# Square roots ahead of an exponential, and two products ahead of a barrier, in a one-core DeltaNet and short-convolution step

## The reference, cut to what matters

```
q, k = l2norm(silu(conv(x W_q))), l2norm(silu(conv(x W_k)));  v = silu(conv(x W_v));  z = x W_z
norm of a token  = sqrt(sum(t*t) + eps)            # per head, q and k
decay            = exp(gc_i - gc_j)                # inside the triangular inverse of each chunk
S, o             = gated delta rule over chunks (prompt), over 8 tokens (each sample)
o                = rmsnorm(o) * norm_g * silu(z)
y                = o @ w_out                       # "the mixer's output projection"
x                = layer_norm(ALPHA * x + y)
```

## Time and profile before

| what | value |
|---|---|
| median of 3 runs | 1735.3 us |
| the profiled execution | 1735.66 us, of which the span is 1733.6 us |
| PE busy | 1692.2 us, 98% |
| DVE busy | 1075.4 us, 62% |
| ACT busy | 460.7 us, 27% |
| POOL busy | 241.5 us, 14% |
| mean granted clock of PE | 0.995 of full speed |

### The profile page before, as it was taken

The page is one execution under the profiler, slowest core; times in us unless marked ns, Lnnn a source line. Parts: engine busy times, 40 slices in busy tenths (PEclk is TensorE's granted clock), DMA queues, the critical chain, the costliest instruction groups (busy, mean ns, idle before and its releaser), DMA issues. The chain is left out here.

```text
span 1733.6 us, 22781 instructions
## 1 busy us (share of the span) xinstructions
PE 1692.2 (98%) x8243; PEld 1321.8 (76%) x8243; DVE 1075.4 (62%) x2062; ACT 460.7 (27%) x1084; POOL 241.5 (14%) x537
## 2 busy tenths in 40 slices
PE   8999999999899999999999999999999999999999
PEld 5777678877677777777777777776777777777777
DVE  4866775676876766662336655468766667633375
ACT  2433406742422222210033111114222222200051
POOL 0111216652110000001100000012100000001100
PEclk9999999989999999999999999999999999999999
DMA  4232210331222222242140322211222222321211
GB/s 155 74 115 87 82 61 14 111 124 37 72 73 79 79 86 73 74 144 83 50 135 1 115 80 83 75 49 50 73 73 74 85 78 81 139 96 67 86 49 55
DMA packets 45645, 139.40 MB, mean 80 GB/s; under 512 B 4944, under 2 KB 12240, under 8 KB 45536
## 3 DMA queue, kind: packets, MB, share of 16 engines
q1 hardware_dynamic: 42864, 133.36, 23.6%
q10 hardware_dynamic: 2672, 4.61, 0.8%
HBM read 129.63 MB, written 8.31 MB: 80 GB/s over the span
## 5 line engine op out<-in xcount | busy, mean ns | idle before, releaser
L274 PE MATMUL bank<-z,ring 128*128 128x288 f32 x1952 | 509.5, 408 | 10.2 <-DVE z L392 2.8
L274 PEld LDWEIGHTS bank<-z,ring 128*128 128x128 f32 x1952 | 370.9, 191 | 117.8 <-issue 8.0
L274 PE MATMUL bank<-x,ring 128*128 128x288 f32 x1632 | 428.0, 409 | 11.4 <-DMA x<-in_x 4.9
L274 PEld LDWEIGHTS bank<-x,ring 128*128 128x128 f32 x1632 | 310.3, 191 | 102.0 <-issue 6.6
L2191 DVE SCALAR_TENSOR_TENSOR scratch<-scratch 128x592 f32<-128x592 f32 x176 | 146.2, 832 | 25.6 <-ACT scratch L2135 24.0
L274 PE MATMUL bank<-y,ring 128*128 128x288 f32 x616 | 156.4, 406 | 0.0
L274 PE MATMUL bank<-big,ring 128*128 128x288 f32 x536 | 137.8, 412 | 4.5 <-PEq L1774 2.3
L274 PEld LDWEIGHTS bank<-y,ring 128*128 128x128 f32 x616 | 117.0, 190 | 32.3
L274 PEld LDWEIGHTS bank<-big,ring 128*128 128x128 f32 x536 | 102.9, 193 | 35.4 <-issue 5.0
L2135 ACT ACTIVATE scratch<-scratch 128x592 f32<-128x592 f32 x88 | 69.4, 789 | 90.7 <-DVE scratch L2165 89.1
L2225 POOL COPY scratch<-scratch 128x2 f32<-128x2 f32 x88 | 26.0, 296 | 465.8 <-ACT scratch L2121 465.8
(11 more groups left out here) (372 smaller groups left out, 2172.4 us busy)
## 6 DMA issues: line engine op xcount, KB each, us to landing
ring<-in_w_up SPq DMA_DIRECT2D x88, 512.0 KB, 3.6
ring<-in_w_scin SPq DMA_DIRECT2D x24, 512.0 KB, 3.6
ring<-in_w_qkv SPq DMA_DIRECT2D x21, 512.0 KB, 3.6
ring<-in_w_down SPq DMA_DIRECT2D x12, 704.0 KB, 4.1
scratch<-in_w_down SPq DMA_DIRECT2D x12, 704.0 KB, 5.4
ring<-in_w_z SPq DMA_DIRECT2D x8, 512.0 KB, 3.6
big<-in_st_S SPq DMA_DIRECT2D x16, 256.0 KB, 6.0
out_dn_S_sample<-big SPq DMA_DIRECT2D x16, 256.0 KB, 3.0
```

The lines of the kernel that those rows point to most:

```text
L274: last = pe.matmul(bank[:, 0:HALF], w[:, k * P:(k + 1) * P], rhs(k), start=start and k == 0, stop=k == self.depth - 1, skip_group_check=no ...
```

## The change

Three edits. First, on ScalarE in block 1, the three square roots now stand ahead of the Exp of the inverse's decay. Second, the first products p1(0) and p1(1) of the output projection go from the head of block 3 to the end of block 2's TensorE order, behind the last update. They read 288 prompt columns and weights that block 1 loaded. Third, to keep banks 0 and 1 free for them, the updates of heads 6 and 7 and the second turn use other banks, and wait for other states.

```diff
-        UPDATE_BANKS = ((0, 1), (2, 3), (0, 1), (2, 3), (4, 5), (6, 7), (2, 3), (4, 5))
+        UPDATE_BANKS = ((0, 1), (2, 3), (0, 1), (2, 3), (4, 5), (6, 7), (4, 5), (6, 7))
+        TURN_BANKS = (0, 2)
...
-                pe.wait_ge(self.s_out, nth_update(2, 1))
+                pe.wait_ge(self.s_out, nth_update(3, 0))
                 self.turn_pe(pe, 1)
-                pe.wait_ge(self.s_out, nth_update(3, 1))
+                pe.wait_ge(self.s_out, nth_update(4, 1))
                 self.update_pe(pe, 6)
-                pe.wait_ge(self.s_out, nth_update(4, 1))
+                pe.wait_ge(self.s_out, nth_update(5, 1))
                 self.update_pe(pe, 7)
...
-            act.wait_ge(i_arg, NBL + 1)
-            act.activation(INV_G, INV_G, ACT.Exp).then_inc(i_expd, 1)
             act.wait_ge(turned, 1)
             act.activation(NRM[:, 0:NCH, :], BANK[6][:, 0:NCH * NT].rearrange("p (c m) -> p c m", m=NT), ACT.Sqrt
                            ).then_inc(rooted, 1)
             for part, c in ((slice(0, SAMP), NCH), (slice(SAMP, P), NCH + 1)):
                 act.activation(NRM[part, NCH, :], BANK[6][part, c * NT:(c + 1) * NT], ACT.Sqrt).then_inc(rooted, 1)
+            act.wait_ge(i_arg, NBL + 1)
+            act.activation(INV_G, INV_G, ACT.Exp).then_inc(i_expd, 1)
...
+        dout_first = Dense(NPAIR, KH, ring_set, lambda i, block: ring_loaded(uses[2] + 1, i, block),
+                           lambda k: BIG[:, 3 * k + 1, :], None, 0)
...
                 prompt.pe(pe)
                 samples.pe(pe)
+                dout_first.p1(pe, 0)
+                dout_first.p1(pe, 1)
...
         def mixer_pe(pe):
-            end_products(pe, dout, None, None, lambda pe: None, None)
+            d = dout
+            d.p2(pe, 0)
+            d.p2(pe, 1)
+            for i in range(2):
+                d.p6(pe, i)
+            for i in range(2):
+                d.p7(pe, i)
+            for i in range(2):
+                d.p4(pe, i)
+            end_products_late(pe, d)
             norm[0].sums(pe, 0)
             end_products_last(pe, dout)
```

More of the change, by code:

```diff
@@ L888, in turn_pe @@
                 for h in range(group * GROUP, (group + 1) * GROUP):
-                    last = pe.transpose(SBANK[group][:, h % GROUP * SAMP:(h % GROUP + 1) * SAMP], S_OS[B, h, :], IDENT[B, B])
+                    last = pe.transpose(SBANK[TURN_BANKS[group]][:, h % GROUP * SAMP:(h % GROUP + 1) * SAMP], S_OS[B, h, :], IDENT[B, B])
                 last.then_inc(self.o_turned, 1)
@@ L976, in gate_dve @@
                 dve.scalar_tensor_tensor(out=BIG[:, 1:QKV_T:3, SEQ:TOK][:, heads], scalar=norm_g,
-                                         in0=SBANK[group][:, 0:GROUP * SAMP].rearrange("p (h t) -> p h t", h=GROUP),
+                                         in0=SBANK[TURN_BANKS[group]][:, 0:GROUP * SAMP].rearrange("p (h t) -> p h t", h=GROUP),
                                          in1=Z[:, heads, SEQ:TOK], op0=ALU.mult, op1=ALU.mult).then_inc(self.o_gated, 1)
```

## The result

Before 1735.3 us (5 runs, 1732.45 to 1737.86), after 1742.0 us (5 runs, 1740.11 to 1742.41): ratio 1.0035, 95% interval [1.0023, 1.0047]. The change makes the kernel slower by 0.2 to 0.5%. The profiled execution took 1742.41 us (span 1740.5), 6.9 us of span more than the one of before. Ten more runs of the changed kernel, taken later beside 33 of the kernel before, gave 1740.05 against 1735.06, ratio 1.003 [1.0019, 1.004].

A forecast was written before the change was run, and what follows sets the result against it. TensorE, busy 98% of the span, was taken to bound the kernel. 1735.66 - 0.67 + 0 + 3.75 = 1738.7, less 0.4 to the median: 1738.4 us; own range 1737.6 to 1739.4, whole range 1734.9 to 1741.2.

The forecast's parts named there:

- rival 1: Block 3: the clock falls again behind TensorE's new gap, costing 1.7 us more, 1740.1 us; chance 0.22.
- Edit 2, 0: End of the samples' rule: new banks and waits hold up no update; cost 0, at most 0.4 us.
- Edit 3, +3.75: Second barrier: early products open it later, VectorE's u1(0) comes late, p7(0) waits; +3.75 us, between +1.55 and +5.45.
- The clock behind the new idle time: Block 3, behind TensorE's 3.8 us gap: forecast counts no clock fall; a fall would cost 1.7 us.
- Edit 1, -0.67: Block 1 grams: roots fit ScalarE's idle time, TensorE's wait for them goes; -0.67 us, between -2.4 and 0.
- rival 5: Block 1 grams: moving the roots gives nothing, the issue gap being fixed in time; 1739.1 us, chance 0.10.
- Rival 4: Second barrier: products fill TensorE's 2.26 us stand and the clock rises 1.7 us earlier; 1730.7 us, chance 0.07.

The follow-up runs named there:

- e3: Kernel before with only the other banks and waits for the updates of heads 6 and 7 and the second turn: 1735.7 us, ratio 0.9999.
- e2: Kernel before with the other banks and waits and the two products ahead of the barrier, square roots left behind the exponential: 1739.81 us, ratio 1.0023.
- e5: Changed kernel with VectorE's six weight sums of pairs 0 and 1 also ahead of the barrier: 1733.06 us, ratio 0.9992 to the kernel before.
- e4: Changed kernel with six extra unused matmuls in TensorE's gap before p7(0): 1739.93 us, ratio 1.0021 to the kernel before.
- e1: Kernel before with only the square roots moved ahead of the exponential on ScalarE: 1735.91 us against 1736.16, ratio 1.0.
- e7: Kernel before with dense matmuls between all three groups of 64 gram records: median 1731.08 us from 1734.37, ratio interval [0.9972, 1.0035].
- e6: Kernel before with only the first 64 gram records split off by dense matmuls, 128 left in a row: 1736.63 us, ratio 1.0007.
- e8: Changed kernel with both p2, ScalarE's copies of p1, six weight sums and all 16 token sums also ahead of the barrier: 1735.07 us, ratio 0.9999.
- e11: Changed kernel with p2, ScalarE's copies, weight sums and p6's token sums ahead of the barrier, other token sums behind u1(1): 1734.25 us, ratio 0.9997.
- e10: Changed kernel with VectorE's six weight sums ahead of the barrier and dense matmuls between the three gram groups: 1728.9 us, ratio 0.9968 to the kernel before.
- e12: Changed kernel with VectorE's sums divided around the barrier, p2 and copies ahead, and grams spread among dense matmuls: 1729.26 us, ratio 0.9965.

## Why the prediction was wrong

The result, 1742.0 us, lies above the range (1734.9 to 1741.2); the median of the later runs, 1740.05, lies within it, near rival 1 (1740.1). Whether the time fell inside or outside was thus partly chance; the step that failed below is seen in the traces of both.

- **Edit 2, 0.** Right: e3 shows no change, and in the traces of after and e3 no wait of the updates appears. In e2, where the updates ran at full clock, one waits 0.28 us; the prediction had up to 0.4 for that case.
- **Edit 3, +3.75.** Right in mechanism and size. The products took 5.99 us (6.1 predicted), the barrier opened at 388.8, of which 0.8 came from block 1, u1(0) came 13.8 us behind it, and TensorE waited 3.66 for it (3.8 predicted). p7(0) starts at 402.75, less 0.8 it is 3.9 later than 398.05. That the size fits so well is partly luck: it holds where the updates run at half clock, and in e2, where they didn't, it is 2.8. e5 shows the cause: with the six sums ahead of the barrier the loss goes.
- **The clock behind the new idle time: the step that failed.** The forecast had no fall there, and gave it to rival 1 at 0.22. It fell, in the traces of after (both) and of e2, and e4 sizes it at 1.6 to 1.7 us, as the rival had it. The comparison that I leant on was the stretch at 457 in the earlier trace rows, with 1.79 us of matmuls in 3.4. No idle time there is longer than 1.78 us, so it was no likeness of a gap of 3.8. Nor is it a place where the clock is sure to stay up: behind the same waits it falls in four of the 14 traces (0.54 from 459 to 462 us in e1, 0.50 from 453 to 456 in e7, and in e4 and e6). The nearer row was the fall at 214.8, behind a stand of 3.06 us in dense work, like the new gap. The Trainium skill, "TensorE: Matmul & The Clock Gate", section "Why this matters for your kernels", warns of such pauses, and the traces agree in this place.
- **Edit 1, -0.67.** The working on ScalarE was right: the roots fit in its idle time, and the exponential stayed at 206.3. The value was wrong: rival 5 (0.10), the wait gives nothing because the stand ends when it does, took place, and beyond it the low clock lasted longer, +0.8 in the trace of after, where the end of the range for this edit was 0. In medians e1 shows nothing either way.

By these terms: 1735.66 + 0.8 + 0 + 3.9 + 1.8 + 0.4 = 1742.6 beside the 1742.41 of the profiled execution (the spans differ by 6.9). The two misses have one thing in common: I treated two idle times of TensorE as worth their own length, and each also decided the clock of the dense work behind it. Rivals 1 and 5 together give 1740.8, still within the range. What takes the first result out of it is what no term had: the longer low clock in block 1 (0.8 where 0 was the worst) and the 0.4 behind the sums.

Rival 4 hoped for the 2.26 us at the barrier and 1.7 of clock, if VectorE had slack. e5, e8 and e11 give VectorE's work three other places and win 0.1 to 0.7 us in that stretch, no more than it varies by itself. The reason is in the earlier trace rows: VectorE ends the states at 382.92 and has 13.77 us of work to u1(0), so with all of that work ahead of it u1(0) can't come before 396.7, and TensorE asked at 398.05: 1.35 us was all that could be had.

What stays open is why the median of e7 lies only 3.3 us below before when its stretch in block 1 gives 4.6. In e10 and e12 the two agree: 5.5 and 5.1 us in medians, 5.4 in the stretch of each. One part may be the clock elsewhere, as the fall in e7 from 453 to 456 us, where before, e10 and e12 have none behind the same waits; one trace can't say how often it falls there.

## What to carry to other kernels

Before you move one engine's work ahead of a barrier, ask which engine is late behind it. If that is another one whose queue is full from the barrier on, the move delays it by its own length, unless its work goes ahead too. And price an idle time of TensorE with the clock of the dense work behind it: here a wait of 3.7 us cost another 1.7. A stall that the profile calls issue is worth as much attention as a wait: the largest gain of this study, 5.0 us in medians between e11 and e12, came from spreading 192 short records among dense ones.

## What the runs showed of the hardware

- **Short matmuls in a row can run out of instructions.** 189 grams at about 11 ns each, then a stand of 2.47 to 3.80 us, before the same three records in each of the kernels with over 64 in a row, whether TensorE had waited 0.7 us in between or not. It ends 1.3 to 1.6 us behind a packet of 16 KB on the instruction queue. With 64 in a row, and 4.15 us of dense matmuls between the groups, there is none. The Trainium skill, "Runtime: NRT & Kernel Launch", section "Instruction fetch mechanics", says that instructions are refilled in blocks of 256 and that the cost of crossing is mostly hidden. For the size (one packet for 250 records) and for the dense stretches the traces agree: from 218.73 to 262.30 us before, TensorE never stands, with a packet at 240.12. In the grams the cost isn't hidden.
- **The same kernel varies with its clock.** The kernel before took 1731.46 to 1737.86 us in 33 runs on one chip. The fastest had a mean granted clock of 0.997, the slowest one of 0.993. The traces differ in where the clock is low: from 27 to 30 us it was at 0.50 in the one of before and at 1.00 in e1, and the grams came 1.7 us sooner.
- **A table load runs ahead of its activation's wait.** It is at 204.44 in the trace of after, and the exponential that it serves waits for VectorE until 206.34. So the two switches of tables, moved into idle time, cost nothing here: the exponential starts 0.12 us later than before.
